# Late attention projections in narrower chunks, spread between the heads of the layer; two banks for the transposed weights

## The chip, the cores and the metric

The kernel runs on one core of one Trainium2 chip. The metric is the device time of one execution in microseconds (us); lower is better.

## The reference, cut to what matters

Six transformer layers run one after the other on 256 tokens of width 1024, in float32. Layers 0 and 1 are a hybrid mixer (pooling, chunk attention, stick-breaking attention) with a dense feed-forward layer and a mixture of eight experts. Layers 2 to 5 are attention layers, each followed by a squared-ReLU feed-forward layer of width 4096:

```
layer 2, 5: diff_attention    16 score heads of 64, values 128 wide, one normalisation per pair of heads
layer 3:    moba_attention    16 heads of 64
layer 4:    swa_sink_attention 16 query heads, 2 key/value heads, a bias on the projection, window 128
each:  qkv = h @ w_in ; rope on q and k ; s = q k^T ; p = softmax(s) ; o = p v ; h += o @ w_out
       h += relu(rms_norm(h) @ w_up)^2 @ w_down
```

## The kernel before, in words

Every float32 matrix product is made of three products of rounded parts: ScalarE (ACT) writes the high part `whi` of a weight unit (1 MB, 128x2048), VectorE (DVE) the low part `wlo`, and TensorE (PE) multiplies high by high, low by high and high by low. Weight units come in order through a ring of six load slots (`NR`), four of which have a high part (`NH`). So unit u+4 can be split only when unit u is used up; `hi` and `lo` are these splits, and in the heads they are done in two halves each.

The projection of a layer is cut into chunks of columns (`CHUNKS`, line 43). The first ones are computed by `project`; the last `LATE` ones are cut into parts, one (chunk, unit, half of the tokens t) each, which `soft_heads` places between the heads. A part of 512 columns is 12 matmuls. The heads are a software pipeline over steps i = 0 to n+3. At an even step PE turns q and k of a pair of heads (`turn_heads`), at an odd step it computes the scores of that pair (`pair_scores`); at each step it transposes the softmax weights of head i-3 (L1341) and multiplies head i-4 with its values (`values`). ACT copies q and k (`copy_qk`), computes the exponentials of head i-2 and, in layers 2 and 5, copies the transposed weights to `pt`; in layers 3 and 4 DVE does that copy (L2165). DVE also applies mask and maximum to the scores (L2154) and finishes the outputs (`finish_group`). Each engine walks its own list of steps in program order, so an instruction that waits holds back all that follow it on its engine.

Before the change the late parts of layers 2, 3 and 5 are eight, one in each of steps 0 to 7, and in layer 4 four in steps 0 to 3. The steps after these have no projection in them: they are called bare below. The two halves of each split stand at steps given by `late_used`: in layers 2, 3 and 5 at (2,3), (4,5), (6,7) and (8,12), in layer 4 at (2,3) and (6,9). The late projections accumulate in banks 3 and 5 (one for each half of the tokens). The transposed weights go to bank 4 alone until the late parts are over and then to banks 4 and 5 in turn (`pt_bank`). Results are evacuated from the bank by ACT (`evacuate`, L1497), in layer 4 by DVE with the bias (`add_bias`, L2056).

`project` in the PE list (L784) computes chunk 0 and 1 for t = 0, with the transposes of the second half of the tokens (`turn(3 * l, 1)`) just ahead of the last unit of chunk 1, and then chunk 0 and 1 for t = 1. Those transposes need the normalised second half of the tokens.

Of the kernel before, what the change touches and what calls it, by code (L numbers as in the profile page):

```python
# [16 lines left out]
NT = S // P  # L17
# [153 lines left out]
def build(nc, A, out, bias_scratch):  # L171
    with ExitStack() as ctx:
# [248 lines left out]
        def late_parts(l):  # L421

            return 2 * LATE[KIND[l]] * len(PLAN.proj[l][-1])

        def late_part(l, p):

            n = 2 * len(PLAN.proj[l][-1])
            return first_late(l) + p // n, p % n // 2, p % 2

        def late_used(l, i):  # L430


            n = late_parts(l)
            last = {HYB: (5, 6), SWA: (3, 6)}.get(KIND[l], (1, 5))
            return [(PLAN.proj[l][late_part(l, p)[0]][late_part(l, p)[1]], half) for p in range(1, n, 2)
                    for half in range(2) if i - p == (last if p == n - 1 else (1, 2))[half]]
# [14 lines left out]
        def turn_bank(l, j):  # L451
# [3 lines left out]
            return bank[2 if j <= late_parts(l) else 2 + j // 2 % 2]  # L455
# [10 lines left out]
        def pt_bank(l, j):  # L466
            return bank[4 if j + 3 <= late_parts(l) else 4 + j % 2]
# [182 lines left out]
        def _(pool):  # L650
# [58 lines left out]
        def _(pe):  # L709
# [122 lines left out]
            def project_late(l, p):  # L832
                c, j, t = late_part(l, p)
                if c > first_late(l) and j == 0:
                    pe.wait_ge(proj_ev, proj_at(l, c - 1, t))
                project_part(l, c, j, t)
# [457 lines left out]
            def soft_heads(l):  # L1294

                kind = KIND[l]
                n, dv, og, late = NSOFT[kind], VW[kind], OGRP[kind], late_parts(l)
                for i in range(n + 4):
                    if i == 0:
                        project_late(l, 0)  # L1300
# [9 lines left out]
                    if i == late + 2:  # L1310

                        pe.wait_ge(proj_ev, EV0[l + 1])
                    if i == 8 and kind == SWA:
                        pe.wait_ge(late_rope_done, 1)
# [6 lines left out]
                    if i == 1:  # L1321
# [3 lines left out]
                        project_late(l, 1)  # L1325
                    if i % 2 == 1 and i < n:
                        pair_scores(l, i - 1)
                    if 1 < i < late:
                        project_late(l, i)
                        if kind == HYB:  # L1330
                            if i == 2:

                                pe.wait_ge(proj_ev, proj_at(l, 4, 1))
                            stick_values(l, i - 1)
# [105 lines left out]
        def _(act):  # L1440
# [127 lines left out]
            def soft_heads(l):  # L1568
                kind = KIND[l]
                n = NSOFT[kind]  # L1570
                for i in range(max(n + (3 if kind == DIFF else 2), late_parts(l) + 6)):
# [23 lines left out]
                    if i < late_parts(l):  # L1595
                        c, j, t = late_part(l, i)
# [216 lines left out]
        def _(dve):  # L1813
# [318 lines left out]
            def soft_heads(l):  # L2132
# [8 lines left out]
                for i in range(n + 4):  # L2141
# [15 lines left out]
                    if i < late_parts(l):  # L2157
# [8 lines left out]
                    if i >= late_parts(l) and kind != HYB:  # L2166
# [12 lines left out]
                    if i < late_parts(l):  # L2179
# [387 lines left out]
```

## Time and profile before

| what | us |
|---|---|
| median of 3 runs | 2504.95 (2501.95 to 2507.85) |
| the profiled execution | 2504.93 |
| its span in the trace | 2503.1 |
| PE busy in the span | 2439.6 (97%) |
| DVE busy | 1697.6 (68%) |
| ACT busy | 1436.1 (57%) |

Busy PE is not PE at its peak: the end of a matmul is modelled and covers part of the gap behind it. In the heads the start times of the weight loads (PEld) tell more. A line of the timeline has the start in us, the duration in us (from the first start to the last end of what is merged), the engine, the line of the kernel, the operation, what it writes and reads, and in brackets the idle time before it with what ended it.

### The profile page before, as it was taken

Reading aid. Unit: us, or ns where it says so; the run is one execution under the profiler, and the core shown is the slowest. Engines: PE = TensorE matmul, PEld = TensorE weight load, DVE = VectorE, ACT = ScalarE, POOL = GpSimd, SP = SyncE. Lnnn points to the kernel's source line nnn. Section 1 sums busy time; section 2 is a strip of 40 time slices with the busy share of each in tenths; the row PEclk is TensorE's granted clock in tenths of the full one; section 3 lists DMA queues with packets and bytes.
Section 4 is the critical chain, followed back from the end, with each engine's and each line's share of the span. In section 5 each row is a group of like instructions: output and inputs, shape, how many; then the busy total and the mean of one; then the engine's idle time right before and its main releaser. Section 6 shows DMA issues by size and latency. Waiting matters only on the chain. (4 is left out here: it accounts for less than half of the span.)

```text
span 2503.1 us, 33592 instructions
## 1 busy us (share of the span) xinstructions
PE 2439.6 (97%) x13444; PEld 2083.8 (83%) x13444; DVE 1697.6 (68%) x1817; ACT 1436.1 (57%) x1603; POOL 83.9 (3%) x94
## 2 busy tenths in 40 slices
PE   8999999999999999999999999999999999999998
PEld 6889978788888888888878789878898789887897
DVE  4665466788888898888975754565546665557554
ACT  5344353588888888887845544453444544455442
POOL 0000010000000000000000200000000000003000
PEclk9999999999999999999999999998999999999999
DMA  8256552599999999999955265452655165552552
GB/s 307 68 199 204 186 190 70 212 353 348 346 339 347 336 346 351 334 350 335 351 195 205 84 217 190 164 186 69 220 190 189 59 208 185 184 194 87 192 185 101
DMA packets 241907, 555.49 MB, mean 222 GB/s; under 512 B 10761, under 2 KB 36769, under 8 KB 241441
## 3 DMA queue, kind: packets, MB, share of 16 engines
q1 hardware_dynamic: 241696, 552.40, 64.0%
q8 instruction: 166, 2.72, 0.4%
q14 instruction: 45, 0.36, 0.0%
HBM read 551.30 MB, written 1.07 MB: 221 GB/s over the span
## 5 line engine op out<-in xcount | busy, mean ns | idle before, releaser
L1830 DVE TENSOR_TENSOR wlo<-raw,whi 128x2048 fp32r<-128x2048 f32 x488 | 1117.3, 2297 | 468.7 <-ACT whi L1460 468.2
L1460 ACT ACTIVATE whi<-raw 128x2048 fp32r<-128x2048 f32 x488 | 935.5, 1924 | 576.0 <-issue 147.1
L931 PE MATMUL bank<-xt_hi,whi 128*128 128x256 f32 x1056 | 299.4, 284 | 0.0
L931 PE MATMUL bank<-xt_hi,wlo 128*128 128x256 f32 x1056 | 299.4, 283 | 0.0
L931 PE MATMUL bank<-xt_lo,whi 128*128 128x256 f32 x1056 | 299.3, 283 | 0.0
L777 PE MATMUL bank<-whi,xt_hi 128*128 128x512 f32 (+1 forms) x528 | 204.4, 387 | 6.4 <-DVE wlo L1836 3.0
L931 PEld LDWEIGHTS bank<-xt_lo,whi 128*128 128x128 f32 x1056 | 200.9, 190 | 1.3
L931 PEld LDWEIGHTS bank<-xt_hi,whi 128*128 128x128 f32 x1056 | 200.9, 190 | 1.1
L931 PEld LDWEIGHTS bank<-xt_hi,wlo 128*128 128x128 f32 x1056 | 200.9, 190 | 0.0
L777 PE MATMUL bank<-wlo,xt_hi 128*128 128x512 f32 (+1 forms) x528 | 198.9, 377 | 0.0
L777 PE MATMUL bank<-whi,xt_lo 128*128 128x512 f32 (+1 forms) x528 | 198.8, 376 | 0.0
L845 PE MATMUL bank<-whi,h_hi 128*128 128x512 f32 x600 | 186.7, 392 | 0.0
L845 PE MATMUL bank<-whi,h_lo 128*128 128x512 f32 x600 | 186.5, 392 | 0.0
L845 PE MATMUL bank<-wlo,h_hi 128*128 128x512 f32 x600 | 186.5, 392 | 0.0
L1087 PE MATMUL bank<-whi,xt_hi 128*128 128x512 f32 (+1 forms) x384 | 144.6, 377 | 3.5 <-DVE wlo L1830 2.6
L1087 PE MATMUL bank<-whi,odd_hi 128*128 128x512 f32 (+1 forms) x384 | 145.1, 378 | 2.8 <-DVE wlo L1830 2.8
L1087 PE MATMUL bank<-wlo,odd_hi 128*128 128x512 f32 (+1 forms) x384 | 143.9, 375 | 0.0
L1087 PE MATMUL bank<-whi,odd_lo 128*128 128x512 f32 (+1 forms) x384 | 143.5, 374 | 0.0
L1087 PE MATMUL bank<-wlo,xt_hi 128*128 128x512 f32 (+1 forms) x384 | 143.3, 373 | 0.0
L1087 PE MATMUL bank<-whi,xt_lo 128*128 128x512 f32 (+1 forms) x384 | 143.0, 372 | 0.0
L845 PEld LDWEIGHTS bank<-wlo,h_hi 128*128 128x128 f32 x600 | 112.8, 188 | 24.9
L845 PEld LDWEIGHTS bank<-whi,h_lo 128*128 128x128 f32 x600 | 112.9, 188 | 24.2
(304 smaller groups left out, 4039.3 us busy)
## 6 DMA issues: line engine op xcount, KB each, us to landing
raw<-in_moe_wg SPq DMA_DIRECT2D x88, 1024.0 KB, 5.9
raw<-in_moe_wu SPq DMA_DIRECT2D x88, 1024.0 KB, 5.9
raw<-in_moe_wd SPq DMA_DIRECT2D x88, 1024.0 KB, 5.7
raw<-in_mlp_w_up SPq DMA_DIRECT2D x64, 1024.0 KB, 5.3
raw<-in_mlp_w_down SPq DMA_DIRECT2D x64, 1024.0 KB, 4.9
raw<-in_diff_w_in SPq DMA_DIRECT2D x24, 1024.0 KB, 5.5
raw<-in_w_in SPq DMA_DIRECT2D x19, 1024.0 KB, 7.8
raw<-in_moba_w_in SPq DMA_DIRECT2D x12, 1024.0 KB, 5.1
```

The costliest lines, as they stand in the source:

```text
L777: mm = pe.matmul(proj_bank(l, c, t)[:, 0:width], a[:, kx, t * P:(t + 1) * P], b[:, k, :], start=(kx == 0 and i == 0), stop=(kx == KT - 1 a ...
L845: mm = pe.matmul(bank[4 + 2 * t + half][:, :], a[:, k, t * P:(t + 1) * P], b[:, kk, half * 512:(half + 1) * 512], start=begin and i == 0, ...
L931: mm = pe.matmul(bank[b + f // 2][:, f % 2 * S:(f % 2 + 1) * S], w[:, k, f * P:(f + 1) * P], a[:, kx, :], start=(kx == 0 and i == 0 and f ...
L1087: mm = pe.matmul(bank[b][:, 0:width], a[:, kx, t * P:(t + 1) * P], w[:, k, :], start=(kx == 0 and i == 0), stop=(kx == KT - 1 and i == 2))
L1460: act.activation(whi[u % NH][:, :], raw[u % NR][:, :], ACT.Copy).then_inc(hi_ready[u % NR], 2)
L1830: dve.tensor_tensor(wlo[u % NR][:, :], raw[u % NR][:, :], whi[u % NH][:, :].bitcast(F32), ALU.subtract).then_inc(lo_ready[u % NR], 2)
```

## The change

For layers 2, 3 and 5 the last chunk of 512 columns becomes two of 256, so that three chunks are late instead of two; the eight parts stand at steps 0, 1, 2, 3, 5, 8, 11 and 13. For layer 4 both chunks of 512 columns become two of 256 each; three chunks are late instead of one, in six parts at steps 0, 0, 1, 2, 5 and 8. The halves of the splits move with them. A chunk is now computed first for t = 0 and then for t = 1, and nearly all late chunks use bank 3 alone, so that t = 1 waits for the evacuation of t = 0. Bank 5 is then free for the transposed weights from the first head on. In layer 4 the early rotary part on DVE covers 4 query heads instead of 8 and GpSimd (POOL) rotates the other twelve in three pieces. The two hybrid layers keep their order.

```diff
-          DIFF: [(0, 512), (1024, 512), (512, 512), (1536, 512), (2048, 512), (2560, 512)],
-          MOBA: [(0, 512), (1024, 512), (512, 512), (1536, 512), (2048, 512), (2560, 512)],
-          SWA: [(1024, 256), (0, 512), (512, 512)]}
-LATE = {HYB: 2, DIFF: 2, MOBA: 2, SWA: 1}
+          DIFF: [(0, 512), (1024, 512), (512, 512), (1536, 512), (2048, 512), (2560, 256), (2816, 256)],
+          MOBA: [(0, 512), (1024, 512), (512, 512), (1536, 512), (2048, 512), (2560, 256), (2816, 256)],
+          SWA: [(1024, 256), (0, 256), (256, 256), (512, 256), (768, 256)]}
+LATE = {HYB: 2, DIFF: 3, MOBA: 3, SWA: 3}
+LATE_STEPS = {HYB: (0, 1, 2, 3), DIFF: (0, 1, 2, 3, 5, 8, 11, 13), MOBA: (0, 1, 2, 3, 5, 8, 11, 13),
+              SWA: (0, 0, 1, 2, 5, 8)}
+SPLIT_STEPS = {HYB: ((2, 3), (8, 9)), DIFF: ((3, 4), (5, 6), (9, 10), (14, 16)),
+               MOBA: ((3, 4), (5, 6), (9, 10), (14, 16)), SWA: ((2, 3), (4, 6), (9, 10))}
-         SWA: [[(16, 2)], [(0, 8)]], HYB: []}
+         SWA: [[(16, 2)], [(0, 4)]], HYB: []}
...
-                return bank[(3, 5)[t]]
+                return bank[(3, 5)[t] if KIND[l] == HYB or KIND[l] == SWA and c == first_late(l) else 3]
...
+        def late_list(l):
+            return [(c, j, t) for c in range(first_late(l), len(CHUNKS[KIND[l]])) for t in range(NT)
+                    for j in range(len(PLAN.proj[l][c]))]
...
-            return bank[2 if j <= late_parts(l) else 2 + j // 2 % 2]
+            return bank[2]
...
-            return bank[4 if j + 3 <= late_parts(l) else 4 + j % 2]
+            return bank[4 if KIND[l] == HYB and j <= 1 else 4 + j % 2]
...
-                    pool.wait_ge(proj_ev, EV0[l + 1])
-                    rotate(pool, link, [(8, 8)], late_tmp).then_inc(late_rope_done, 1)
+                    for r in range(3):
+                        pool.wait_ge(proj_ev, proj_at(l, 2 + r, 1))
+                        rotate(pool, link, [(4 + 4 * r, 4)], late_tmp[:, r % 2 * 256:]).then_inc(late_rope_done, 1)
...
+            def project_late(l, c, j, t):
+                if KIND[l] == HYB and c > first_late(l):
                     pe.wait_ge(proj_ev, proj_at(l, c - 1, t))
+                elif KIND[l] != HYB and j == 0 and (c > first_late(l) or t == 1 and KIND[l] != SWA):
+                    pe.wait_ge(proj_ev, proj_at(l, c, t) - 1)
+                elif KIND[l] == SWA and t == 1:
+                    pe.wait_ge(proj_ev, proj_at(l, 1, 0))
                 project_part(l, c, j, t)
...
-                            pe.wait_ge(pt_ready, s if i <= late + 2 else s - 1)
+                            pe.wait_ge(pt_ready, s if kind == HYB and i <= 6 else s - 1)
...
+                        if j in (8, 12) and kind in (DIFF, MOBA):
+                            pe.wait_ge(proj_ev, proj_at(l, 5 + (j - 8) // 4, 1))
```

## Rows read from the trace of the kernel before

**Rows 1.** The page: busy time, share and instructions of each engine.

```profile
PE 2439.6 (97%) x13444; PEld 2083.8 (83%) x13444; DVE 1697.6 (68%) x1817; ACT 1436.1 (57%) x1603; POOL 83.9 (3%) x94
```

**Rows 2.** Windows, the heads of layers 5, 3, 4: engines busy, granted clock, DMA share, GB/s.

```profile
2236.18:2288.78 52.60, 49.37 (x334) 40.45 (x333) 38.35 (x144) 36.00 (x103) 14.94 (x18) 1.00 0.29 96
...
1653.10:1711.66 58.56, 55.77 (x334) 46.77 (x332) 35.94 (x109) 30.25 (x87) 0.00 (x0) 0.85 0.26 86
...
1940.22:1982.36 42.14, 38.08 (x284) 31.05 (x284) 31.79 (x99) 26.74 (x94) 2.56 (x6) 1.00 0.17 56
```

**Rows 3.** Timeline of PE's weight loads, layer 5: pairs in bare steps, first `out_project` matmul.

```profile
2265.85 0.47 PEld L1290 LDWEIGHTS bank<-cst,h_qkv 128*128 128x128 f32 x4
...
2274.67 0.47 PEld L1290 LDWEIGHTS bank<-cst,h_qkv 128*128 128x128 f32 x4
...
2278.22 0.47 PEld L1290 LDWEIGHTS bank<-cst,h_qkv 128*128 128x128 f32 x4
...
2282.76 0.36 PEld L1342 LDWEIGHTS bank<-cst,z 128*128 128x128 f32 x3
...
2288.78 0.30 PEld L845 LDWEIGHTS bank<-whi,xt_hi 128*128 128x128 f32 x2
```

**Rows 4.** The same view, layer 3: steps 8 and 10, a long wait, first `out_project` matmul.

```profile
1682.52 0.48 PEld L1290 LDWEIGHTS bank<-cst,h_qkv 128*128 128x128 f32 x4
...
1685.86 0.48 PEld L1290 LDWEIGHTS bank<-cst,h_qkv 128*128 128x128 f32 x4
1688.64 0.32 PEld L1342 LDWEIGHTS bank<-cst,z 128*128 128x128 f32 x3 [2.30 <-ACT z L1583]
...
1711.66 0.30 PEld L845 LDWEIGHTS bank<-whi,xt_hi 128*128 128x128 f32 x2
```

**Rows 5.** Windows of PE, layer 3: PE busy, granted clock, DMA share, GB/s.

```profile
1692.00:1704.00 12.00, 12.00 (x60) 0.50 0.00 0
...
1706.00:1708.00 2.00, 2.00 (x19) 0.93 0.00 0
```

**Rows 6.** Timeline of ACT and DVE, layer 3, step 8: the halves of one split.

```profile
1684.65 1.04 ACT L1464 ACTIVATE whi<-raw 128x1024 fp32r<-128x1024 f32 x1
...
1685.72 1.23 DVE L1836 TENSOR_TENSOR wlo<-raw,whi 128x1024 fp32r<-128x1024 f32 x1 [1.36 <-ACT whi L1464]
```

**Rows 7.** Chain that ended last, feed-forward of layer 4: 96 matmuls of 256, 48 of 512 columns.

```profile
2042.49 11.50 PE bank L931 x96
2053.99 10.99 PE bank L845 x48
```

**Rows 8.** Timeline of PEld and ACT, layer 5, step 3.

```profile
2247.41 0.47 PEld L1342 LDWEIGHTS bank<-cst,z 128*128 128x128 f32 x3
...
2248.55 1.05 ACT L1464 ACTIVATE whi<-raw 128x1024 fp32r<-128x1024 f32 x1
2249.50 0.59 ACT L1497 ACTIVATE h_qkv<-bank 128x512 f32<-128x512 f32 x1
```

**Rows 9.** Timeline of PEld and DVE, layer 4: its first matmul to its first heads.

```profile
1918.25 0.19 PEld L777 LDWEIGHTS bank<-whi,xt_hi 128*128 128x128 f32 x1
...
1922.89 1.28 DVE L1936 SCALAR_TENSOR_TENSOR y<-x,rstd,gain 128x1024 f32<-128x1024 f32 x1 [0.66 <-POOL rstd L659]
...
1924.22 0.86 PEld L720 LDWEIGHTS bank<-cst,y 128*128 128x128 f32 x8 [0.39 <-DVE y L1936]
...
1940.22 0.42 PEld L1290 LDWEIGHTS bank<-cst,h_qkv 128*128 128x128 f32 x4 [1.50 <-DVE h_qkv L508]
```

**Rows 10.** Timeline of DVE, layer 4: one 256-column evacuation; first and last score instruction of step 1.

```profile
1931.00 0.42 DVE L2056 TENSOR_TENSOR h_qkv<-bank,swa_bias 128x256 f32<-128x256 f32 x1 [2.18 <-PE bank L777]
...
1944.63 0.35 DVE L2154 CUSTOM_DVE_ANT_0 z<-bank,cst,minus_sinks 128x128 f32<-128x128 f32 x1 [2.17 <-issue]
...
1945.98 0.08 DVE L2154 DVE_READ_ACCUMULATOR2_ANT nmx<- 128x1 f32 x1
```

**Rows 11.** Windows of PE, layer 0, a fall of the clock inside projection matmuls.

```profile
43.70:48.00 4.30, 4.30 (x14) 0.60 1.10 348
```

More of the change, by code:

```diff
@@ L419, in last_units, with late_units, late_at @@
             return PLAN.down[l][n - 2] + PLAN.down[l][n - 1]
[L421 to L428, printed above, removed]
+        def late_units(l):
+            return [(c, j) for c in range(first_late(l), len(CHUNKS[KIND[l]])) for j in range(len(PLAN.proj[l][c]))]
+        def late_list(l):
+            return [(c, j, t) for c in range(first_late(l), len(CHUNKS[KIND[l]])) for t in range(NT)
+                    for j in range(len(PLAN.proj[l][c]))]
+        def late_at(l, i):
+            return [part for part, at in zip(late_list(l), LATE_STEPS[KIND[l]]) if at == i]
         def late_used(l, i):
[L433 to L436, printed above, removed]
+            return [(PLAN.proj[l][c][j], half) for (c, j), steps in zip(late_units(l), SPLIT_STEPS[KIND[l]])
+                    for half in range(2) if steps[half] == i]
         def stick_z(p):
@@ L1296, in soft_heads @@
                 kind = KIND[l]
-                n, dv, og, late = NSOFT[kind], VW[kind], OGRP[kind], late_parts(l)
+                n, dv, og = NSOFT[kind], VW[kind], OGRP[kind]
                 for i in range(n + 4):
                     if i == 0:
-                        project_late(l, 0)
+                        for part in late_at(l, 0):
+                            project_late(l, *part)
                         if kind == HYB:
@@ L1309, in soft_heads @@
                         pe.wait_ge(pool_read, l + 1)
-                    if i == late + 2:
+                    if i == 6 and kind == HYB:
                         pe.wait_ge(proj_ev, EV0[l + 1])
-                    if i == 8 and kind == SWA:
-                        pe.wait_ge(late_rope_done, 1)
+                    if i in (4, 8, 12) and kind == SWA:
+                        pe.wait_ge(late_rope_done, i // 4)
                     elif i == 8 and kind != HYB:
@@ L1324, in soft_heads @@
                             pe.wait_ge(arg_ready, STICK0[l] + NSTICK[HYB])
-                        project_late(l, 1)
+                        for part in late_at(l, 1):
+                            project_late(l, *part)
                     if i % 2 == 1 and i < n:
                         pair_scores(l, i - 1)
[L1328 to L1334, printed above, removed]
+                    if i > 1:
+                        for part in late_at(l, i):
+                            project_late(l, *part)
+                    if i in (2, 3) and kind == HYB:
+                        if i == 2:
+                            pe.wait_ge(proj_ev, proj_at(l, 4, 1))
+                        stick_values(l, i - 1)
                     j = i - 3
@@ L1570, in soft_heads @@
                 n = NSOFT[kind]
-                for i in range(max(n + (3 if kind == DIFF else 2), late_parts(l) + 6)):
+                for i in range(max(n + (3 if kind == DIFF else 2), 10)):
                     if i < n and i % 2 == 0:
@@ L1594, in soft_heads @@
                         hi(u + NH, (half,))
-                    if i < late_parts(l):
-                        c, j, t = late_part(l, i)
+                    for c, j, t in late_at(l, i):
                         if j == len(PLAN.proj[l][c]) - 1:
@@ L2156, in soft_heads @@
                             ins.then_inc(z_read, 1)
-                    if i < late_parts(l):
+                    if i < 4 if kind == HYB else late_at(l, i):
                         for u, half in late_used(l, i):
@@ L2165, in soft_heads @@
                         dve.tensor_copy(pt[:, s % 4], pt_bank(l, j)[:, 0:384]).then_inc(pt_ready, 1)
-                    if i >= late_parts(l) and kind != HYB:
+                    if kind != HYB and not late_at(l, i):
                         for u, half in late_used(l, i):
@@ L2178, in soft_heads @@
                         finish_group(l, NSTICK[kind] + j, True)
-                    if i < late_parts(l):
-                        c, j, t = late_part(l, i)
-                        if j == 1:
-                            add_bias(l, c, t)
+                    for c, j, t in late_at(l, i):
+                        add_bias(l, c, t)
                 if kind == HYB:
```

3 lines of the change are left out of this document (removed).

## The prediction

> **What bounds the kernel now.** I read the page first: PE is busy 97% of the span [rows 1], so only what PE issues, waits for, or does at a lower clock can move the end. Next I cut the heads of the changed layers out with windows [rows 2]. There DVE has 38.4 of 52.6 us and ACT 36.0; neither is a bound by its total, but in a bare step they are nearly as loaded as PE. The timeline of PE's weight loads then shows what PE loses. In layer 5 the last four pairs of heads take 16.9 us (2265.85 to 2282.76), the quickest of them 3.55 us, so 2.7 us over four times that; the tail behind them takes 6.0 us [rows 3]. In layer 3 the stretch is 6 us longer than in layer 5 and the mean granted clock is 0.85 [rows 2]: after a wait of 2.30 us at step 10 [rows 4] the clock is granted at 0.50, which is 1.2 of 2.4 GHz, over some 17 us [rows 5]. Layer 2 looks like layer 5, row by row. The DMA share in the heads is 0.17 to 0.29 [rows 2], so where weights are loaded doesn't matter here.
>
> **The change part by part.** Sums are made against the profiled execution, 2504.93 us, which equals the median, 2504.95.
>
> *Hybrid layers.* Their parts, halves and banks come out the same. Nothing.
>
> *Narrower matmuls.* 96 matmuls of 256 columns take 11.50 us where 48 of 512 take 10.99 [rows 7]: 0.5 us for each chunk cut in two. One in layers 2, 3 and 5, two in layer 4: +2.5 us in all, all on PE, with no cover. It is booked with the layers below. Loads of 256-column units are new in layers 2, 3 and 5. A late one is bounded by nothing lost and by a wait like the longest in [rows 4], 2.3 us; the DMA share of 0.29 [rows 2] is nearer to nothing, which I take.
>
> *Layers 2 and 5.* Four parts go from steps 4 to 7 to steps 5, 8, 11 and 13. A part is work that PE can do whatever ACT and DVE are at, so it hides lateness of the step before it. I walked the steps with the durations of layer 5.
> - Step 4 is now bare. `values` of head 0 needs the evacuation of the 2048 chunk, and on ACT that stands behind the `pt` copy and a half split of step 3. In the trace it ends at 2249.50 + 0.59 = 2250.1; without a part PE would be through with transposes, `turn_heads` and transposes at 2248.65 (1.24 us after 2247.41) [rows 8]. New wait 1.6 us. Bounds: nothing, if ACT gets ahead in step 2, which has lost a half; 2.5 us if the half at step 4 got in first.
> - Of the 2.7 us lost in bare pairs the walk leaves 2.1: 0.7 at step 7 and 0.6 at step 11 (`copy_qk` behind a half), 0.8 at step 16 behind the half of step 14. Gain 0.6, at most 2.7.
> - The half at step 16 is in the tail, ahead of the exponential of head 15, and costs 1.05 us on ACT as in [rows 8], of which some is idle already: +0.3, at most 1.
> Sum with 0.5 for the narrow chunk: +1.8 each, +3.6 for both, from -2 to +8.
>
> *Layer 3.* From 1685.86 to 1711.66 are 25.8 us for three pairs and the tail. At full clock a pair takes 3.34 us (1682.52 to 1685.86) [rows 4] and the tail 6.0 as in layer 5: 16.0. So 9.8 us are lost, 2.3 in the wait and the rest at the half clock. The wait comes from the half split in bare step 8: DVE waits for ACT's 1.04 us, spends 1.23 on the low part [rows 6] and only then takes the scores. In the new order the halves of 4, 6, 9 and 10 have a part in the next step or the one after it, so they are hidden; those of 14 and 16 are not. The walk (`pt` copies on DVE) gives waits of 0.6 in all up to step 12, 0.6 and 1.95 at step 16 and 0.7 more than layer 5 in the tail: 3.9 us, and 0.5 for the chunk. If the clock stays up: -9.8 + 4.4 = -5.4; I take -5, since a walk leaves short gaps out. Bounds: -9 (no new waits) and +1 (the fall comes back as long as it was).
>
> Two banks for the transposes take nothing off here: transposes of head 7 start earlier, but `values` of head 6 behind them needs the same copy of DVE. Worth 0 to 0.6 us in layer 4, steps 3 to 6, and booked there. `turn_bank` on one bank adds a wait on a copy for which `pair_scores` has waited already: nothing.
>
> *Layer 4.* Three things.
> - Entry. `turn(3 * l, 1)` waits for DVE's y, ready at 1922.89 + 1.28, and starts at 1924.22. Chunk 0 of 256 columns and one unit of chunk 1 now cover that wait, and 0.39 us are left. With chunk 1 a single unit only chunk 0 (24 matmuls, 2.9 us from 1918.25) stands ahead of it [rows 9]: the wait grows to 3.1 us. Then come 24 matmuls each for chunk 1, t = 0, chunks 0 and 1, t = 1, and the two parts of step 0: 5 x 2.88 = 14.4 from 1924.22 + 0.86, so the heads start at 1939.4 and the 1.50 us of [rows 9] is gone. Against 1940.22 that is 0.8 sooner, but four parts of 2.88 are left instead of three of 2.75, 3.3 us more: +2.5.
> - Bank 3 alone. The part of step 2 waits until DVE has evacuated the part of step 1, and in DVE's list that stands behind the scores of step 1: from the start of the scores' instructions 1.4 us and 0.42 for the evacuation [rows 10], while PE has only 0.44 of `turn_heads` to do. About +1.8. The part of step 1 waits 0.5 for the second evacuation of step 0. Bounds for both: 1 and 3.
> - Bare steps. The part at 5 hides the halves of 4 and the part at 8 that of 6, which costs 1.6 us now; the half at 10 makes it again. The single-bank waits go (-0.5). Together about -0.6.
> Sum +4.2, from +1 to +7. The rotary pieces on POOL are wanted at steps 4, 8 and 12 and have several steps each: nothing; if a piece is late, some 3 us.
>
> Total: +3.6 - 5 + 4.2 = +2.8, so 2507.7 us.
>
> One rule of the Trainium skill speaks for another result. The trace shows layer 3's clock at half after a wait of 2.30 us among transposes [rows 4, 5], and at full in layer 5, where the waits are shorter. The page TensorE: Matmul & The Clock Gate, section "HAM oscillation — how this bites in real kernels", says that a burst of matmuls followed by idle time puts the array back to its lower clock, and that it pays to keep the dense work together with no idle between. By it spreading the dense parts should keep the clock up; that is the first rival, whose price is from rows.
>
> **The rivals.**
> - *The clock stays up and the new waits don't show.* ACT and DVE run ahead more than in my walk: layer 3 gains 8, layers 2 and 5 gain 1 each, layer 4 loses only its entry, +2.5. -7.5: 2497.5. For it: DVE and ACT have over 14 us free in each stretch [rows 2]. Against: the order on each engine is fixed, and the waits at step 4, at the entry and on bank 3 follow from it.
> - *New falls of the clock (ends slower).* Place: layers 2 and 5, step 4. PE does from 2247.41 only transposes, then waits till 2250.2, 2.8 us without a matmul; in layer 3 the fall came after 3.0 such us (1685.86 to 1688.92). If the clock falls there it stays at half through the bare steps. Price of such a fall: 25.8 - 16.0 - 2.3 = 7.5 us [rows 4] where bare steps follow, 0.40 x 4.3 = 1.7 us where projection matmuls follow at once [rows 11]. Step 5 has a part, so some 4 us each: 2507.7 + 8 = 2516. It decides as soon as the clock falls in one of them.
> - *The fall of layer 3 comes back in its tail*, at step 16, where the walk has 2.9 us without a matmul. `out_project` follows in 6 us, so it costs 3 rather than 7.5: 2511.
> - *No change*: gain and loss cancel to under 1 us, 2505. The narrow chunks alone make +2.5, so a true zero is chance.
>
> **How the numbers follow.** Forecast (2504 to 2510) 0.40, first rival 0.20, new falls 0.16, fall in the tail 0.20, no change 0.04. The range goes from the first rival to the second: 2497 to 2517. The likeliest case alone has 2503 to 2511. 0.2% is 5 us, about what a measurement can tell here. Faster by more is the first rival: 0.20. Slower by more holds the new falls, the fall in the tail and a small part of the forecast: 0.38. Within: 0.42.
>
> **What would show it.** In layers 2 and 5 a wait of about 1.6 us ahead of the first L1389 that ACT's L1497 ends; in layer 4 some 3 us ahead of L720 and a wait on L2056 ahead of the third late part; in layer 3 a heads stretch near 53 us with clock 1.00. I am wrong if the clock of layer 3 is still at 0.5 for 17 us, if layers 2 and 5 get shorter, or if layer 4 does.

## The result, and the profile after

The changed kernel takes 2514.47 us (median of 19 runs, 2510.68 to 2521.95) where the kernel before takes 2507.56 (19 runs, 2501.16 to 2512.32) on the same chip: ratio 1.0033, 95% interval 1.0026 to 1.0041, so 6.9 us slower. The profiled execution took 2512.13 us, 7.2 more than the one before. All sums below are made between the two profiled executions.

The page after says as little as the one before [rows 1]: PE is busy 2442.6 us, 97% of the span.

The windows of the stretches between landmarks say where the time went. After, in this order: heads of layer 5, of layer 3, the entry of layer 4 (first projection matmul to first heads), its heads, the heads of layer 2 and the start of its `out_project`. The columns are those of [rows 2].

```profile
2241.09:2295.24 54.15, 49.92 (x382) 43.09 (x381) 38.75 (x143) 36.22 (x105) 15.85 (x18) 1.00 0.27 93
1656.74:1708.46 51.72, 48.97 (x382) 42.81 (x380) 35.38 (x109) 30.66 (x89) 0.00 (x0) 1.00 0.28 97
1915.03:1939.04 24.01, 19.99 (x154) 19.74 (x153) 16.98 (x30) 8.00 (x8) 0.54 (x1) 0.93 0.52 179
1939.04:1987.30 48.26, 43.10 (x347) 37.52 (x345) 32.73 (x103) 28.64 (x96) 5.27 (x18) 0.96 0.20 67
1347.25:1401.68 54.43, 50.20 (x382) 43.40 (x381) 39.03 (x144) 37.55 (x106) 15.85 (x18) 0.99 0.27 94
1401.68:1405.60 3.92, 3.92 (x13) 3.13 (x13) 3.68 (x12) 0.00 (x0) 2.03 (x3) 0.65 0.00 0
```

| stretch | before | after | difference | forecast |
|---|---|---|---|---|
| up to the heads of layer 2 | | | +0.9 | 0 |
| layer 2, heads | 52.46 | 54.43 | +2.0 | +1.8 |
| behind them | | | +0.8 | 0 |
| layer 3, heads | 58.56 | 51.72 | -6.8 | -5 |
| layer 4, entry | 21.97 | 24.01 | +2.0 | -0.8 |
| layer 4, heads | 42.14 | 48.26 | +6.1 | +5.0 |
| layer 5, heads | 52.60 | 54.15 | +1.6 | +1.8 |
| behind them | | | +0.7 | 0 |
| sum | | | +7.2 | +2.8 |

The heads of layer 2 before are the window 1346.36 to 1398.82; the other values of before are in, or are differences of, [rows 2, 9]. The differences are rounded one by one. The 0.9 at the top lies ahead of the first changed heads and shows what two executions differ by. A landmark is the start of a weight load.

PE's waits are read in the timeline, which has in brackets the idle time before an instruction and what ended it. After, layer 5: ACT and PE in steps 3 and 4, one 256-column part from its first load (L783) to the next load behind it, two of the three waits ahead of the transposes of steps 16 to 18, and the wait behind `out_project`. L1354, L1403, L1478, L1511 and L783 are L1342, L1389, L1464, L1497 and L777 of before.

```profile
2253.46 1.05 ACT L1478 ACTIVATE whi<-raw 128x1024 fp32r<-128x1024 f32 x1
2254.41 0.59 ACT L1511 ACTIVATE h_qkv<-bank 128x512 f32<-128x512 f32 x1
2255.04 0.30 PEld L1403 LDWEIGHTS bank<-h_qkv,pt 128*128 128x128 f32 x2 [1.49 <-ACT h_qkv L1511]
2256.76 0.19 PEld L783 LDWEIGHTS bank<-whi,xt_hi 128*128 128x128 f32 x1 [0.33 <-issue]
2259.63 0.35 PEld L1354 LDWEIGHTS bank<-cst,z 128*128 128x128 f32 x3
...
2287.89 0.31 PEld L1354 LDWEIGHTS bank<-cst,z 128*128 128x128 f32 x3 [0.94 <-ACT z L1597]
...
2293.45 0.31 PEld L1354 LDWEIGHTS bank<-cst,z 128*128 128x128 f32 x3 [2.04 <-ACT z L1597]
2302.45 0.42 PEld L742 LDWEIGHTS bank<-cst,y 128*128 128x128 f32 x4 [1.43 <-POOL y L688]
```

The first pair of lines is step 3's half split with the evacuation of the 2048 chunk right behind it, and PE idle for 1.49 us until that is done, where the walk in [rows 8] had 1.6. The third wait of the steps 16 to 18 is 0.44 us, at 2290.29. The last, 2.04 us, stands ahead of the transposes of head 15: on ACT the half of step 16 and the copies of `turn_mixed` are ahead of the exponential of that head. Before the change this wait was 1.09 us with the copies alone, so the half adds 0.95. Layer 2 has the same four waits.

After, layer 4, same view: the entry down to L726 (L720 of before), then the heads.

```profile
1915.03 0.19 PEld L783 LDWEIGHTS bank<-whi,xt_hi 128*128 128x128 f32 x1
...
1917.18 1.91 ACT L1474 ACTIVATE whi<-raw 128x2048 fp32r<-128x2048 f32 x1 [2.03 <-DMA raw<-in_swa_w_in]
...
1920.97 1.28 DVE L1949 SCALAR_TENSOR_TENSOR y<-x,rstd,gain 128x1024 f32<-128x1024 f32 x1 [0.66 <-POOL rstd L664]
1922.31 0.86 PEld L726 LDWEIGHTS bank<-cst,y 128*128 128x128 f32 x8 [4.22 <-DVE y L1949]
...
1943.86 0.35 DVE L2167 CUSTOM_DVE_ANT_0 z<-bank,cst,minus_sinks 128x128 f32<-128x128 f32 x1 [4.10 <-PE bank L1382]
1945.21 0.42 DVE L2069 TENSOR_TENSOR h_qkv<-bank,swa_bias 128x256 f32<-128x256 f32 x1
1945.69 0.19 PEld L783 LDWEIGHTS bank<-whi,xt_hi 128*128 128x128 f32 x1 [1.51 <-DVE h_qkv L2069]
1951.68 0.30 PEld L1403 LDWEIGHTS bank<-h_qkv,pt 128*128 128x128 f32 x2 [1.01 <-issue]
1973.21 0.30 PEld L1403 LDWEIGHTS bank<-h_qkv,pt 128*128 128x128 f32 x2 [1.71 <-DVE pt L2178]
```

From 1915.03, chunk 0 alone covers the normalisation of the second half of the tokens, and PE waits 4.22 us for it. In the heads, the evacuation L2069 stands behind the scores of step 1 on DVE (L2167) and PE's next part waits 1.51 us for bank 3. The 1.71 us are the half at step 10.

The same view of layer 3 after: its three longest waits.

```profile
1701.14 0.31 PEld L1354 LDWEIGHTS bank<-cst,z 128*128 128x128 f32 x3 [0.62 <-ACT z L1597]
1703.12 0.30 PEld L1403 LDWEIGHTS bank<-h_qkv,pt 128*128 128x128 f32 x2 [1.67 <-issue]
1706.49 0.31 PEld L1354 LDWEIGHTS bank<-cst,z 128*128 128x128 f32 x3 [0.80 <-ACT z L1597]
```

The 2.30 us of [rows 4] are gone, and the clock stays at 1.00. But it now falls elsewhere. Behind the heads of layer 2 it is at 0.65 over 3.92 us (the last window above). Windows of PE after (columns as in [rows 5]), in the entry of layer 4 and behind the 1.71 us in its heads:

```profile
1924.00:1926.00 2.00, 2.00 (x12) 0.50 0.00 0
1974.00:1976.00 2.00, 2.00 (x13) 0.62 0.02 4
1976.00:1978.00 2.00, 2.00 (x12) 0.53 0.00 0
```

### The profile page after: what moved, and what is told of

The parts are those of the page before. It is cut to its first block, busy times and chain, and to the rows that moved or that the text cites. A ratio compares the mean times of both kernels' runs of the same rounds, so it can differ in the third digit from the quotient of the medians.

```text
span 2510.3 us, 34103 instructions
## 1 busy us (share of the span) xinstructions
PE 2442.6 (97%) x13684; PEld 2096.8 (84%) x13684; DVE 1701.6 (68%) x1822; ACT 1437.3 (57%) x1610; POOL 86.3 (3%) x106
## 4 chain that ended last, share of the span: by engine, by line
PE 72%; DVE 5%; ACT 3%; issue 2%; DMA 1%; POOL 0%; DVEq 0%; POOLq 0%; ACTq 0%
PE bank L854 17%; PE bank L1096 16%; PE bank L940 11%; PE bank L783 9%; PE bank L1174 8%; PE bank L957 4%; DVE wlo L1843 2%; ACT whi L1474 2%; PE bank L1068 1%; DMA raw<-in_moe_wu 1%; PE bank L1155 1%; PE bank L1354 1%; PE bank L726 1%; PE bank L1382 1%; PE bank L1380 1%
## 5 line engine op out<-in xcount | busy, mean ns | idle before, releaser
L783 PE MATMUL bank<-whi,xt_hi 128*128 128x512 f32 (+1 forms) x608 | 218.6, 360 | 7.8 <-DVE wlo L1849 3.0
L783 PE MATMUL bank<-wlo,xt_hi 128*128 128x512 f32 (+1 forms) x608 | 213.0, 350 | 0.0
L783 PE MATMUL bank<-whi,xt_lo 128*128 128x512 f32 (+1 forms) x608 | 212.8, 350 | 0.0
L1096 PE MATMUL bank<-whi,xt_hi 128*128 128x512 f32 (+1 forms) x384 | 144.5, 376 | 4.2 <-DVE wlo L1843 3.2
L1096 PE MATMUL bank<-wlo,xt_hi 128*128 128x512 f32 (+1 forms) x384 | 143.2, 373 | 0.0
L1096 PE MATMUL bank<-whi,xt_lo 128*128 128x512 f32 (+1 forms) x384 | 142.8, 372 | 0.0
L783 PEld LDWEIGHTS bank<-whi,xt_hi 128*128 128x128 f32 x608 | 116.3, 191 | 29.3 <-issue 9.4
```

The lines of the kernel that those rows point to most:

```text
L783: mm = pe.matmul(proj_bank(l, c, t)[:, 0:width], a[:, kx, t * P:(t + 1) * P], b[:, k, :], start=(kx == 0 and i == 0), stop=(kx == KT - 1 a ...
L1096: mm = pe.matmul(bank[b][:, 0:width], a[:, kx, t * P:(t + 1) * P], w[:, k, :], start=(kx == 0 and i == 0), stop=(kx == KT - 1 and i == 2))
```

## The experiments

The kernels below hold the steps of parts and halves in the tables `LATE_STEPS` and `SPLIT_STEPS` and can have each kind of layer in the form before or after; with all three in one form they are the kernel before or the kernel after. Ratios are against the kernel before, on the same chip, with 95% intervals. The runs were spread over several chips, so two changed kernels are compared by their ratios and not by their microseconds.

**One layer kind at a time.** Theory: the layers are separate costs, and their sum is the whole. Edit: only layer 3, only layer 4, or only layers 2 and 5 in the new form.

```diff
-OLD = {DIFF, MOBA, SWA}      # all as before
+OLD = {DIFF, SWA}            # layer 3 alone is new
+OLD = {DIFF, MOBA}           # layer 4 alone is new
+OLD = {MOBA, SWA}            # layers 2 and 5 alone are new
```

> The kernel before with only layer 3 in the new form (chunks, steps, halves, banks); layers 2, 4 and 5 as before. Theory (the change's loss is the sum of +2.0 and +1.6 in the heads of layers 2 and 5, about +2 behind them, +8.2 in layer 4 and -6.8 in layer 3): heads of layer 3 near 51.7 us at clock 1.00 instead of 58.6, and the kernel about 7 us faster than before. Rival (the clock of layer 3 fell or not by chance, and the change has no part in it): the time stays within 2 us of before, or other runs show the fall again.

2501.08 us (12 runs), ratio 0.9987 (0.9977 to 0.9998): 3.3 us faster (0.5 to 5.8), and not the 7 us of the theory. Windows of its layer 3, the heads and then PE alone at their end:

```profile
1654.48:1708.69 54.21, 52.26 (x382) 46.39 (x380) 35.55 (x109) 30.79 (x89) 0.00 (x0) 0.93 0.27 93
...
1700.00:1708.69 8.69, 7.82 (x38) 0.53 0.01 2
```

The clock fell in the tail, as the third rival had it, although the code of this layer is that of the changed kernel, where it stayed up. With the same waits it falls in one execution and not in another. The difference of 6.8 us between the two profiled executions is thus an extreme: in the three profiles that have this layer in the form before its heads took 58.56, 55.20 and 55.95 us, in the three that have it exactly as changed 51.72, 54.21 and 51.71.

> The kernel before with only layer 4 in the new form. Theory: entry 24.0 us instead of 22.0 (a wait of some 4 us ahead of the transposes, with a fall of the clock behind it), heads 48 us instead of 42; the kernel is 8 us slower than before. Rival (what layer 4 lost was set by the layers ahead of it, whose clock and loads the change had altered): under +4 us.

2511.3 us (12 runs), 1.0022 (1.0011 to 1.0033): 5.5 slower (2.8 to 8.3), which speaks for the theory but leaves the rival's 4 us inside the interval. Its entry and its heads:

```profile
1912.88:1936.03 23.15, 20.02 (x154) 19.77 (x153) 16.97 (x30) 8.10 (x8) 0.54 (x1) 0.93 0.53 184
1936.03:1985.88 49.85, 44.58 (x347) 38.99 (x345) 32.70 (x103) 28.74 (x96) 5.27 (x18) 0.93 0.19 64
```

73.0 us against 72.3 in the changed kernel and 64.1 before. The layer costs 8.9 us between two profiles where the medians say 5.5; it has a clock of 0.93 over 73.0 us here, so some 5 us of the 8.9 are the half clock, by an estimate from these windows. Whether the other eleven executions had as much of it, no profile shows.

> The kernel before with only layers 2 and 5 in the new form. Theory: a wait of 1.5 us at step 4 and one of 2.0 us ahead of the transposes of head 15 in each, the heads 1.5 to 2 us longer each, and 0.7 to 1.3 us more behind them; the kernel +4 to +6 us. Rival (the spread parts fill the bare steps and the tail costs nothing): between -3 and +1 us.

2510.61 us (12 runs), 1.0021 (1.001 to 1.0032): 5.3 slower (2.5 to 8.0), as the theory had it. Heads of its layer 5:

```profile
2240.24:2294.42 54.18, 49.95 (x382) 43.11 (x380) 38.72 (x143) 36.24 (x105) 15.87 (x18) 1.00 0.27 93
```

The waits 1.49, 0.94 and 2.04 are there to the hundredth. The three ratios add up to +0.30%, give or take 0.19, and the whole change has +0.33%. So the sign of each layer kind is shown, and the layers are separate costs as far as these intervals tell.

**What layer 3 really lacked.** Theory: its loss came from the position of a half, at even step 8, not from how the parts lie. Both halves of that split are moved by a step, in the kernel before:

```diff
-SPLIT_STEPS = {... MOBA: ((2, 3), (4, 5), (6, 7), (8, 12)), ...}
+SPLIT_STEPS = {... MOBA: ((2, 3), (4, 5), (6, 7), (9, 13)), ...}
```

> The kernel before, with the two halves of the last split of layer 3 moved from steps 8 and 12 to steps 9 and 13; nothing else. Theory A (the gain of layer 3 comes from where the halves stand, since at an odd step DVE takes the scores before it waits for ACT's half): the wait of 2.3 us at step 10 shrinks below 0.8, the clock stays at 1.00, and the heads take 50 to 52 us, so the kernel is 6 to 9 us faster without any spread part or narrow chunk. Rival B (it takes projection matmuls between the heads to keep the clock up): the clock still falls to 0.50 in layer 3, and the gain is under 3 us.

2496.71 us (5 runs), 0.9961 (0.9946 to 0.9976): some 9 us faster than before (6 to 13), with not one instruction added. Heads of layer 3:

```profile
1654.72:1704.47 49.75, 48.42 (x334) 40.01 (x333) 35.54 (x109) 30.11 (x87) 0.00 (x0) 1.00 0.30 101
```

No wait over 0.80 us is left, and the rival, that it takes projection matmuls between the heads to keep the clock up, is out. What the change gains in layer 3 by itself (3.3 us) is less than two numbers in a table gain. The two halves were not moved one at a time; the wait that went is the one behind the half of step 8.

**The same move everywhere.** Halves at odd steps also in layers 2 and 5, (9,13), and in layer 4, (7,9).

```diff
-SPLIT_STEPS = {... DIFF: (..., (8, 12)), MOBA: (..., (8, 12)), SWA: ((2, 3), (6, 9))}
+SPLIT_STEPS = {... DIFF: (..., (9, 13)), MOBA: (..., (9, 13)), SWA: ((2, 3), (7, 9))}
```

> The kernel before, with the last split's halves at odd steps in all four layers: (9,13) instead of (8,12) in layers 2, 3 and 5, (7,9) instead of (6,9) in layer 4. Theory (a half at an even bare step makes DVE wait for ACT ahead of the scores): beside layer 3 as in the run before (49.8 us), the waits of 0.79 and 0.78 us of layers 2 and 5 and the 1.60 us of layer 4 go; layers 2 and 5 take 51 to 52 us, layer 4 40.5 us, the kernel is 11 to 14 us faster than before. Rival (in layers 2 and 5 the copy of the transposed weights is on ACT, so the half only moves the wait): layers 2 and 5 stay at 52.4 us and the gain is that of layer 3 alone, 9 us.

2500.26 us (11 runs), 0.9974 (0.9964 to 0.9984): 6.5 us faster than before, under the 9 of the rival and the 11 to 14 of the theory. Its interval overlaps that of the last kernel, so the times don't tell the two apart. The theory fell for layers 2 and 5, whose heads grew from 52.5 to 53.6 and from 52.6 to 53.7. Window of layer 5, and PEld, ACT and DVE around its first new wait:

```profile
2233.12:2286.84 53.72, 49.43 (x334) 40.49 (x333) 39.48 (x144) 35.98 (x103) 14.84 (x18) 1.00 0.28 94
```

```profile
2268.49 1.48 DVE L1861 TENSOR_TENSOR wlo<-raw,whi 128x1024 fp32r<-128x1024 f32 x1
2270.77 0.50 ACT L1618 ACTIVATE pt<-bank 128x384 f32<-128x384 f32 x1
2272.02 0.29 DVE L2146 CUSTOM_DVE_ANT_0 o_tmp<-y 128x128 f32<-128x128 f32 x1
2272.66 0.30 PEld L1415 LDWEIGHTS bank<-h_qkv,pt 128*128 128x128 f32 x2 [1.12 <-issue]
```

L1415 is `values`. It needs the `pt` copy of ACT, but that ended at 2271.27. It also needs bank 6 or 7 back from DVE, which frees it at the end of `finish_group` (`o_read`), here at some 2272.3 (L2146). DVE's low part of the half stood just ahead of that group. The profile names no releaser, so this is read from the order of the lists and the times: PE goes on 0.35 us after L2146 has ended, and so it does behind the second new wait, 1.54 us at 2281.31, with L2146 ending at 2280.95. In layers 2 and 5 DVE finishes a group of two heads (`OGRP`) at every odd step from 5 on, in layers 3 and 4 one of four heads, at steps 7, 11, 15 and 19, so in layer 3 steps 9 and 13 have none. Layer 4 was 41.74 with a wait of 0.79 instead of 1.60.

**Odd steps in the changed kernel.** Its last halves from (14,16) to (15,17), in layer 4 from (9,10) to (9,11).

```diff
-SPLIT_STEPS = {... DIFF: (..., (14, 16)), MOBA: (..., (14, 16)), SWA: (..., (9, 10))}
+SPLIT_STEPS = {... DIFF: (..., (15, 17)), MOBA: (..., (15, 17)), SWA: (..., (9, 11))}
```

> The changed kernel with the halves of its last splits moved to odd steps: (15,17) instead of (14,16) in layers 2, 3 and 5, (9,11) instead of (9,10) in layer 4. Theory: the wait of 2.04 us ahead of the transposes of head 15 in layers 2 and 5 falls to 1.1 and the 0.94 us one goes; the heads of layers 2 and 5 take 52 to 52.5 us instead of 54.3, layer 3 50 instead of 51.7, and in layer 4 the wait of 1.71 us and the fall of the clock behind it go (-3 us). In all 6 to 9 us faster than the changed kernel, within 2 us of the kernel before. Rival (the halves of steps 14 and 16 only show because the tail is bare; at 15 and 17 they show as much): under 2 us faster than the changed kernel. If the spreading of the parts is worth anything by itself, layer 3 comes out under 49.8 us, which the old order reaches with its halves at odd steps.

2514.81 us (7 runs), 1.0035 (1.0024 to 1.0046), which can't be told from the changed kernel. Layer 4's heads came down to 46.31, its 1.71 to 0.79, and the clock stayed up in them (in the entry it fell behind a wait of 4.34 us). In layers 2 and 5 the 2.04 became 1.09, but ahead of `out_project` a wait of 1.75 came, and in layer 2 one of 1.69 behind it. Layer 3 got longer than in the changed kernel. Its window and its wait:

```profile
1657.90:1710.93 53.03, 49.50 (x382) 43.32 (x380) 35.47 (x109) 30.56 (x89) 0.00 (x0) 0.98 0.27 95
```

```profile
1709.70 0.50 PEld L1415 LDWEIGHTS bank<-h_qkv,pt 128*128 128x128 f32 x2 [2.84 <-DVE pt L2190]
```

Neither of the two pairs of positions tried in the tail is free; there is no part left there to hide a half behind.

**The waits of step 4 and of bank 3.** Theory: they are only an order on ACT and DVE. The evacuation goes ahead of the half (ACT) and, in step 1 of layer 4, ahead of the scores (DVE).

```diff
-                    for u, half in late_used(l, i):
-                        hi(u + NH, (half,))
+                    if kind == HYB: ...               # as before
 ...                                                   # the evacuations
+                    if kind != HYB:
+                        for u, half in late_used(l, i):
+                            hi(u + NH, (half,))
 ...
+                    if i == 1 and kind == SWA:        # DVE, ahead of the scores
+                        for c, j, t in late_at(l, i):
+                            add_bias(l, c, t)
```

> The changed kernel with evacuations ahead: ACT evacuates a late chunk before it makes the half split of the same step (layers 2, 3, 5), and DVE evacuates the part of step 1 before it takes the scores of that step (layer 4). Theory: the wait of 1.49 us at step 4 of layers 2 and 5 shrinks to 0.5, and the wait of 1.51 us ahead of the part of step 2 of layer 4 goes; 3 to 3.5 us faster than the changed kernel. Rival (the copies of the transposed weights behind these are late next, so the waits move one instruction on): the heads keep their length within 0.3 us.

2518.1 us (6 runs), 1.0056 (1.0042 to 1.007), slower than the changed kernel by 0.23% or 5.8 us. The 1.49 shrank to 0.54 and the 1.51 is gone, so the order was their cause. But much of it came back one instruction on, as the rival said: in layer 5 a new wait of 0.69 stands ahead of the scores of step 5 (54.38 us of heads against 54.15), and in layer 4 the 1.01 of step 4 became 1.39. In layer 3 ACT's half now waits, behind the evacuation, for PE's part (4.12 us), DVE's `pt` copy comes late behind its low part, and the clock falls. Heads of layer 3, then ACT and PEld in layer 3, in layer 4 and in layer 5:

```profile
1656.66:1715.47 58.81, 52.32 (x382) 45.50 (x380) 35.36 (x109) 30.33 (x89) 0.00 (x0) 0.94 0.25 86
```

```profile
1668.30 0.60 ACT L1523 ACTIVATE h_qkv<-bank 128x512 f32<-128x512 f32 x1 [4.12 <-PE bank L792]
1671.63 0.41 PEld L1415 LDWEIGHTS bank<-h_qkv,pt 128*128 128x128 f32 x2 [2.52 <-issue]
...
1958.60 0.30 PEld L1415 LDWEIGHTS bank<-h_qkv,pt 128*128 128x128 f32 x2 [1.39 <-issue]
...
2259.87 0.30 PEld L1415 LDWEIGHTS bank<-h_qkv,pt 128*128 128x128 f32 x2 [0.54 <-ACT h_qkv L1523]
2261.30 0.30 PEld L1392 LDWEIGHTS bank<-qk 64*128 64x128 f32 x4 [0.69 <-ACT qk L1592]
```

**The entry of layer 4.** Theory: the wait comes from chunk 1 being 256 wide and thus a single unit. Chunk 1 gets its 512 columns back; only the last 512 stay cut in two.

```diff
-          SWA: [(1024, 256), (0, 256), (256, 256), (512, 256), (768, 256)]}
+          SWA: [(1024, 256), (0, 512), (512, 256), (768, 256)]}
-LATE = {..., SWA: 3}         LATE_STEPS SWA: (0, 0, 1, 2, 5, 8)   SPLIT_STEPS SWA: ((2, 3), (4, 6), (9, 10))
+LATE = {..., SWA: 2}         LATE_STEPS SWA: (0, 1, 3, 8)         SPLIT_STEPS SWA: ((2, 3), (9, 11))
-         SWA: [[(16, 2)], [(0, 4)]], HYB: []}
+         SWA: [[(16, 2)], [(0, 8)]], HYB: []}
```

> The changed kernel, with chunk 1 of layer 4 again 512 columns wide (two units), so that only columns 512 to 1023 are late, in four parts of 256 columns at steps 0, 1, 3 and 8, halves at (2,3) and (9,11). Theory (the wait of 4.2 us ahead of the transposes and the fall of the clock behind it come from chunk 1 being one unit): the wait falls to about 0.4 us, the entry has clock 1.00 and takes 22 us with one part in it; layer 4 as a whole (first matmul to out_project) takes 65 to 67 us instead of 72.3 and the kernel is 5 to 7 us faster than the changed one. Rival (the 256-column loads of the layer make y late, as the wait for a load on ACT says): the wait stays above 2 us.

2506.0 us (11 runs), 1.0003 (0.9995 to 1.0012): 7 to 8 faster than the changed kernel, with layers 2, 3 and 5 as changed. Entry and heads of layer 4, and the load that waits for y:

```profile
1917.92:1939.88 21.96, 21.03 (x130) 18.53 (x129) 17.62 (x29) 9.92 (x9) 0.55 (x1) 1.00 0.65 233
1939.88:1983.04 43.16, 38.63 (x320) 33.33 (x321) 31.84 (x101) 26.86 (x94) 4.50 (x12) 1.00 0.16 55
```

```profile
1923.89 0.86 PEld L735 LDWEIGHTS bank<-cst,y 128*128 128x128 f32 x8 [0.39 <-DVE y L1961]
```

65.1 us against 72.3. The wait on y is 0.39 us, as before the change, and the clock at 1.00. The heads are 1.0 us longer than before, of which 0.5 is the price of a narrow chunk. The edit takes away the entry's wait and one of the three late chunks together and moves the halves, so it doesn't split the 7 to 8 us between them.

**Spread, but not so late.** On top of that, parts and halves of layers 2, 3 and 5 moved out of the tail.

```diff
-LATE_STEPS DIFF: (0, 1, 2, 3, 5, 8, 11, 13)   SPLIT_STEPS DIFF: ((3, 4), (5, 6), (9, 10), (14, 16))
+LATE_STEPS DIFF: (0, 1, 2, 3, 5, 8, 10, 11)   SPLIT_STEPS DIFF: ((3, 4), (5, 6), (9, 10), (12, 13))
-LATE_STEPS MOBA: (0, 1, 2, 3, 5, 8, 11, 13)   SPLIT_STEPS MOBA: ((3, 4), (5, 6), (9, 10), (14, 16))
+LATE_STEPS MOBA: (0, 1, 2, 3, 5, 7, 9, 11)    SPLIT_STEPS MOBA: ((3, 4), (5, 6), (9, 11), (13, 15))
```

> The changed kernel with layer 4 as in the run with the wide chunk 1, and the late parts of layers 2, 3 and 5 ending two steps earlier, so that no half split is left for the tail: layers 2 and 5 parts at 0, 1, 2, 3, 5, 8, 10, 11 and halves of the last two chunks at (9,10) and (12,13); layer 3 parts at 0, 1, 2, 3, 5, 7, 9, 11 and halves at (9,11) and (13,15). Theory (the waits of the tail come from the half of step 16): the wait ahead of the transposes of head 15 in layers 2 and 5 falls from 2.04 to 1.1, their heads from 54.2 to 53 or less, and layer 3 takes 50 to 50.5 us against 49.7 of the old order with halves at odd steps, the difference being the narrow chunk (0.5 us). So spreading is worth nothing in layer 3. Rival (spread parts do fill waits once the halves are out of the way): layer 3 under 49.5 and layers 2 and 5 under 52.

2503.45 us (11 runs), 0.9988 (0.9979 to 0.9998): some 3 us faster than before (0.5 to 5), with narrow chunks and spread parts in all four layers. The theory held for layer 3 and fell for layers 2 and 5. Heads of layers 3 and 5, and layer 5's waits:

```profile
1656.54:1706.49 49.95, 48.99 (x382) 42.81 (x380) 35.72 (x109) 30.45 (x89) 0.00 (x0) 1.00 0.30 101
2233.55:2288.21 54.66, 50.03 (x382) 43.12 (x381) 38.98 (x144) 36.10 (x105) 14.96 (x18) 1.00 0.28 92
```

```profile
2268.90 0.19 PEld L792 LDWEIGHTS bank<-whi,xt_hi 128*128 128x128 f32 x1 [0.68 <-ACT h_qkv L1523]
...
2282.67 0.30 PEld L1415 LDWEIGHTS bank<-h_qkv,pt 128*128 128x128 f32 x2 [1.21 <-issue]
2286.41 0.31 PEld L1366 LDWEIGHTS bank<-cst,z 128*128 128x128 f32 x3 [1.09 <-ACT z L1609]
```

In layer 3 a good spread reaches 49.95, which is what the unspread order reaches (49.75) plus less than the price of a narrow chunk. In layer 5 the 1.49 stayed and the tail improved (2.04 to 1.09), but as much came back: 0.68 on the single bank and 1.21 ahead of `values`. This last one is again not the `pt` copy, which ended at 2281.47: DVE had a low part from 2279.03 and then the group of heads until 2282.32, again 0.35 us before PE went on.

**The best of what was found**: the kernel before with the halves of layer 3 at (9,13) and of layer 4 at (7,9).

```diff
-SPLIT_STEPS = {... MOBA: (..., (8, 12)), SWA: ((2, 3), (6, 9))}
+SPLIT_STEPS = {... MOBA: (..., (9, 13)), SWA: ((2, 3), (7, 9))}
```

> The kernel before, with only the last split's halves moved where that helped: layer 3 at (9,13) instead of (8,12), layer 4 at (7,9) instead of (6,9); layers 2 and 5 keep (8,12), since odd steps cost them 1.1 us each. Theory: layer 3 49.7 us, layer 4 41.7 us at clock 1.00, layers 2 and 5 52.5 us; the kernel is 8 to 11 us faster than before and at least as fast as the run with layer 3 alone. Rival (what layer 3 gained came with the state of the clock in layer 4 and gives way when that layer's waits change): less than 6 us faster.

2497.4 us (6 runs), 0.9969 (0.9957 to 0.9981): 7.8 us faster than before and, by the two ratios, some 16 faster than the changed kernel. The heads of layer 3 take 49.75 us, as in the run with layer 3 alone; heads of layer 4:

```profile
1930.15:1971.88 41.73, 38.33 (x284) 31.07 (x284) 31.69 (x99) 26.73 (x94) 2.56 (x6) 1.00 0.17 56
```

Layer 4's 0.4 us is in the profile but too small for the medians; this kernel and that with layer 3 alone (0.9961) can't be told apart.

## Why the prediction was right, and where its sizes were off

The forecast was slower by 2.8 us, with the gain in layer 3 eaten by layers 2, 4 and 5. The kernel is slower, by 6.9, and each of the three layer kinds has the sign that it was given. The size is another matter: the change costs more than twice the forecast, 2514.5 us is outside the 2503 to 2511 of the likeliest case, and the 0.42 given to a difference within 5 us did not come. The stated range, 2497 to 2517, holds it because it reaches to the second rival.

The signs that were named came: in layers 2 and 5 a wait ahead of the first `values` that ACT's evacuation ends (1.49), in layer 4 a wait ahead of the transposes (4.22) and one on the bias evacuation ahead of the third late part (1.51), in layer 3 heads of 51.7 us at a clock of 1.00.

**The term that was mis-sized is the clock.** Of the 9.8 us that the sum takes off in layer 3, it puts 7.5 to the half clock, and no layer is charged for a new fall. Every execution has its mean granted clock on record, so its cost can be estimated as (1 - clock) x span. For the kernel before this averages 13.3, 13.7 and 13.9 us on three chips (29, 25 and 16 executions), for the changed kernel 14.9 us (19 executions). So over many executions the change saves nothing on the clock, where 7.5 us were forecast. Outside of the clock the time grew by some 6 to 8 us, where the forecast has 10.3 (2.8 and the 7.5). Two errors, one in each direction, brought the sum as near as it is, and that is luck. In the kernel with layer 3's halves at odd steps the same estimate is 7.0 us (5 executions): there the clock's cost did go down, by some 6 us. The clocks are on record to 0.001, which is 2.5 us, so these averages are good to about 1 us. The part that every execution has at its start and end is in all of them.

Where the miss of 4 us lies can't be told by layer. The two profiles put it into layer 4 (+4.2 in the forecast, +8.2 between them). The runs with one layer kind changed spread it: layer 3 -3.3 for -5, layers 2 and 5 +5.3 for +3.6, layer 4 +5.5 for +4.2, and each forecast lies inside the interval of its run. In detail, from the profiles:

- *Layer 4, entry.* "the wait grows to 3.1 us": it grew to 4.22, and to 3.34 with layer 4 alone changed. The difference is a load: ACT waited 2.03 us for one of the new 256-column units, 1.15 us in the other profile, and its high part stands ahead of the normalisation, so y was ready 7.22 and 6.34 us after the first matmul, against 5.92 in [rows 9]. The prediction bounded such a late load in layers 2, 3 and 5 and took nothing; in layer 4 it didn't ask. Then the clock was at 0.50 for the projection matmuls behind the wait, 0.93 over the stretch or 1.7 us: not in any term. The forecast was -0.8 for the stretch, and +2.0 was measured.
- *Layer 4, heads.* The wait on bank 3, "about +1.8", was 1.51, ended by L2069 as said. The part more, 3.3, can't be measured by itself. "The part at 5 hides the halves of 4 and the part at 8 that of 6": 1.01 us at step 4 remained; the half at 10 made its wait again, 1.71 for 1.6, but the clock fell behind it, which cost 1.7 us. So 6.1 instead of 5.0.
- *Layers 2 and 5.* Step 4: 1.49 for 1.6. The heads together +3.5 for +3.6, but not as the walk had it. Its waits of 0.7 at step 7 and 0.6 at step 11 did not come: up to step 15 nothing but step 4 is over 0.4 us. At step 16 it was 0.94 for 0.8. The tail was charged with +0.3 and got +1.4, from 1.09 to 0.44 and 2.04. These two errors cancel, which is luck too. Not foreseen: +0.8 behind layer 2, where after the 2.04 us the clock fell, and +0.7 behind layer 5, where POOL's y ended a wait of 1.43 instead of 0.71.
- *Layer 3.* -6.8 for -5 between the two profiles; over runs -3.3. The waits left are 0.62, 1.67 and 0.80, 3.1 us, where the walk had 3.9. That the long wait of the kernel before came from where the halves stand is confirmed by the kernel in which they alone were moved: it took away the wait and the fall.
- *Narrower matmuls.* A part of 24 matmuls of 256 columns takes 2.87 us (2256.76 to 2259.63), as taken from [rows 7].
- *Two banks for the transposes, the rotary pieces:* neither was tried alone. No wait over 0.4 us in the changed heads is put down to a rotary piece or to a missing bank for the transposes; the 1.01 us of layer 4 has no releaser named. Bank 3 alone cost 0.68 us in layer 5 where the parts lie close together, and 1.51 in layer 4.

Of the rivals, the first (clock up and no new waits) failed on the waits. The second, new falls in layers 2 and 5 at step 4, did not come: the wait of 1.49 us stands there ten times in five profiles, and the clock stayed at 1.00 each time. Falls of its kind came in other places, after 2.04 us in layer 2 and after 4.22 and 1.71 us in layer 4. The third, a fall in the tail of layer 3, came in one of the three profiles that have this layer exactly as changed. The Trainium skill, TensorE: Matmul & The Clock Gate, section "HAM oscillation — how this bites in real kernels", was quoted for the first rival: idle time after a burst puts the array at its lower clock, so dense work should be kept together. The falls in layers 2 to 5 agree in so far as each begins in or behind idle time of PE, down to the waits of 0.98 us in the last section. That spreading the parts should keep the clock up was the prediction's own reading, and the runs don't bear it out: the spread layer 3 was at 0.53 over its last 8.7 us in one profile, and the unspread one with its wait removed was at 1.00 in all three.

The lesson of the sum: where a wait was priced by one chain of instructions it was priced well (1.49 for 1.6, 1.51 for 1.8, 1.71 for 1.6), and what follows a wait, a clock fall or a moved load, was priced at nothing. Between the two profiles the three falls (some 5 us), the late load (1.1) and the 0.7 behind layer 5, less the 1.8 that layer 3 did better, come to about 5, against the 4.4 by which +7.2 exceeds +2.8. That is a sum of readings, not an experiment, and it leaves out the 0.9 at the top.

## What to carry to other kernels

Before parts are spread to fill gaps, find the one instruction whose position makes the long wait: a weight split in halves is a chain over two engines, and moving its two halves from even to odd steps gained some 9 us where a rebuilt schedule lost 7. Which step is free depends on what else the two engines have in it: the same move was a loss of 1.1 us in the profile of each layer where DVE finishes a group of heads, and frees PE's bank, at every odd step. When a chunk is made narrower, look for what its length covered ahead of a dependent instruction. Charge a new wait amid small matmuls with a share of a fall of the clock, by how often one followed such a wait, and judge a gain that comes from the clock over many executions.

## What the runs showed of the hardware that was not expected

- The length of a fall varies between executions with the same waits. Behind the wait of 2.30 us in layer 3, which all three profiles of its form before have, the heads took 58.56 us with some 17 us at 0.50 [rows 5], and 55.20 and 55.95 at a mean of 0.94 and 0.91.
- Whether the clock falls varies too, and the length of the wait alone doesn't decide it. The table counts, over the entry of layer 4 and the heads of layers 2 to 5 in all twelve profiles, the waits of 1.49 us and more that several kernels share, and of the shorter ones the one behind which falls came:

| wait of PE, place | times | followed by a fall |
|---|---|---|
| 3.34 to 4.49 us, entry of layer 4 | 4 | 4 |
| 2.30 us, layer 3 before, step 10 | 3 | 3 |
| 2.04 us, layers 2 and 5, ahead of head 15 | 8 | 3 |
| 1.71 us, layer 4, behind the half of step 10 | 3 | 2 |
| 1.67 us, layer 3, behind the half of step 14 | 4 | 1 |
| 1.60 us, layer 4 before, behind the half of step 6 | 4 | 1 |
| 1.50 us, end of the entry of layer 4 before | 6 | 0 |
| 1.49 us, layers 2 and 5, step 4 | 10 | 0 |
| 0.98 us, end of the heads of layer 4 | 12 | 3 |

The last row's falls begin at the first `out_project` matmuls, up to 2 us behind the wait. Windows of PE: one of these, one behind the 1.60 us, and one behind the 2.04 us of layer 5 in the changed kernel, where the clock stayed up.

```profile
1979.00:1984.00 5.00, 4.97 (x22) 0.66 0.02 3
...
1956.00:1960.00 4.00, 4.00 (x24) 0.58 0.00 0
...
2293.00:2299.00 6.00, 5.55 (x34) 1.00 0.00 0
```

They are from the kernel with layer 3 alone changed, from the one with its halves at odd steps, and from the changed kernel.
- Loads into narrower chunks came late in the entry of layer 4: ACT waited 2.03, 1.15, 2.14 and 2.30 us for a 1 MB unit of `in_swa_w_in` in the four profiles that have this entry as changed, 0.53 us where chunk 1 is wide again, and for no load there in the kernel before. Whether the 1 KB rows of a 256-column unit are the cause, or the earlier start of the stretch, wasn't tried.
